# Group weights of dilated attention formed on eight rows, three z tiles beside memory attention, and fetches awaited by their reader

## The reference

```python
for gi, (window, dil) in enumerate(DIL_GROUPS):        # (128, 1), (512, 4), (2048, 16)
    num, m, den = dilated_window_group(q, k, v_a, window, dil)
ms = jnp.stack(ms)
wts = jnp.exp(ms - jnp.max(ms, axis=0, keepdims=True))
num = sum(wts[g][..., None] * nums[g] for g in range(3))
den = jnp.sum(wts * jnp.stack(dens), axis=0)
out = num / den[..., None]
...
y = jnp.concatenate([a_out, b_out, m_out], axis=-1) * jax.nn.silu(z)
return x + y @ w_out
```

## Time and profile before

| | |
|---|---|
| runs | 3665.96, 3662.26, 3666.74 us; median 3665.96 us |
| the profiled execution | 3660.47 us, span 3658.7 us |
| mean granted clock of TensorE over the span | 0.974 |
| busy: PE, DVE, ACT, POOL | 3404.2, 1763.5, 931.8, 1503.5 us |
| share of PE in the chain that ended last | 70%, and DVE 11%, POOL 4%, ACT 3% |

### The profile page before, as it was taken

How to read it: one execution, slowest core, us unless ns; L and a number is a source line. 1 busy time by engine, 2 the same in 40 slices (tenths; PEclk the granted TensorE clock), 3 DMA queues, 4 the chain that set the end, 5 groups by cost and what they waited for, 6 DMA issues and landing times.

```text
span 3658.7 us, 44381 instructions
## 1 busy us (share of the span) xinstructions
PE 3404.2 (93%) x16512; PEld 2766.0 (76%) x16512; DVE 1763.5 (48%) x2626; ACT 931.8 (25%) x1810; POOL 1503.5 (41%) x1917
## 2 busy tenths in 40 slices
PE   7989899999999999989999899889888999999988
PEld 6778888887786677767778588778766777788767
DVE  4734887744124454533523556675544443413343
ACT  3233322213014432323112322323220222300121
POOL 2452533243452245534554254354324334434423
PEclk9999999999999999999999999999999999999999
DMA  3121211121131021231222211010122101211211
GB/s 118 46 81 30 88 40 48 51 64 40 52 101 38 27 67 35 58 109 35 57 55 88 71 41 35 24 35 24 46 68 71 55 21 49 67 40 39 80 36 70
DMA packets 298890, 201.19 MB, mean 55 GB/s; under 512 B 25510, under 2 KB 277418, under 8 KB 298698
## 3 DMA queue, kind: packets, MB, share of 16 engines
q1 hardware_dynamic: 271241, 132.77, 13.2%
q10 hardware_dynamic: 27456, 65.76, 4.9%
HBM read 170.96 MB, written 27.54 MB: 54 GB/s over the span
## 4 chain that ended last, share of the span: by engine, by line
PE 70%; DVE 11%; PEld 6%; POOL 4%; issue 3%; ACT 3%; DMA 1%; ACTq 1%; PEldq 0%; DVEq 0%; POOLq 0%; SPq 0%
PE ps L347 53%; PE ps L1637 4%; PEld ps L347 4%; POOL w_lo L3098 2%; PE ps L987 2%; POOL w_hi L3092 1%; PEld ps L2577 1%; PE ps L360 1%; PE ps L1000 1%; PE ps L2066 1%; ACT wrk L1015 1%; PE ps L1930 1%; PE ps L746 1%; PE ps L2473 1%; PE ps L739 1%
## 5 line engine op out<-in xcount | busy, mean ns | idle before, releaser
L3092 POOL TENSOR_TENSOR w_hi<-w_raw,pool_one 128x256 fp32r<-128x256 f32 x908 | 612.7, 703 | 1996.2 <-PE ps L347 1974.2
L347 PE MATMUL ps<-h_hi,w_hi 128*128 128x512 f32 x2928 | 1206.6, 412 | 77.1 <-POOL w_lo L3098 19.5
L347 PE MATMUL ps<-h_hi,w_lo 128*128 128x512 f32 x2928 | 1152.3, 394 | 0.0
L347 PE MATMUL ps<-h_lo,w_hi 128*128 128x512 f32 x2928 | 1151.5, 393 | 0.0
L3098 POOL TENSOR_TENSOR w_lo<-w_raw,w_hi 128x256 fp32r<-128x256 f32 x1004 | 891.3, 916 | 129.7 <-ACT w_hi L1370 108.4
L347 PEld LDWEIGHTS ps<-h_hi,w_hi 128*128 128x128 f32 x2928 | 557.0, 190 | 250.2 <-issue 92.0
L347 PEld LDWEIGHTS ps<-h_hi,w_lo 128*128 128x128 f32 x2928 | 555.4, 190 | 121.4
L347 PEld LDWEIGHTS ps<-h_lo,w_hi 128*128 128x128 f32 x2928 | 557.9, 191 | 107.0 <-issue 6.0
L347 PE MATMUL ps<-y_hi,w_hi 128*128 128x512 f32 x704 | 289.4, 411 | 33.0 <-DVEq L2644 15.9
L347 PE MATMUL ps<-y_hi,w_lo 128*128 128x512 f32 x704 | 277.9, 395 | 0.0
L347 PE MATMUL ps<-y_lo,w_hi 128*128 128x512 f32 x704 | 277.8, 395 | 0.0
(11 more groups left out here) (400 smaller groups left out, 3961.0 us busy)
## 6 DMA issues: line engine op xcount, KB each, us to landing
w_raw<-in_w_in SPq DMA_DIRECT2D x87, 512.0 KB
w_raw<-in_even_w_in SPq DMA_DIRECT2D x48, 512.0 KB
away<-wrk ACTq DMA_DIRECT2D x72, 256.0 KB, 2.0
w_raw<-in_odd_w_in SPq DMA_DIRECT2D x32, 512.0 KB
wrk<-away ACTq DMA_DIRECT2D x24, 512.0 KB
wrk<-in_x ACTq DMA_DIRECT2D x16, 512.0 KB, 8.7
w_raw<-in_w_br SPq DMA_DIRECT2D x32, 256.0 KB
w_raw<-in_even_w_out SPq DMA_DIRECT2D x24, 256.0 KB
```

Of the source, the lines that this page charges most:

```text
L347: mm = nc.tensor.matmul(ps[:, b, 0:n], w[:, slot, k, :], rhs(part, k, b), start=(k == 0 and q == 0), stop=(k == nk - 1 and q == 2))
L3092: ins = nc.gpsimd.tensor_tensor(hi, raw, one[:, 0:2], ALU.mult)
```

## The change

It has four parts. **One:** in dilated attention the six numbers per token stay on 8 partitions. DVE writes them, multiplied with masks (the new constants low4, high4, low16, high16), into tiles of 128x384; four matmuls bring the maxima and four the sums of all three groups onto 8 rows by 384 columns in token order; maximum, difference, exponential, weighted sum and reciprocal are taken there, and 24 matmuls with the identity's columns as weights spread the finished weights to 128 partitions, where DVE multiplies the three outputs from PSUM. All this stands inside the attention's stage, at planned times behind the last slot; the five stages go, and the join keeps two sums, silu of z and the split. SLOT_TIME goes from 2.7 to 4.2. **Two:** in both layers three of the four z tiles stand beside the memory attention, in `first_gates`: ACT copies the halves out and then applies Silu to three whole tiles, and `gates_beside` has DVE's part. The fourth tile is `last_gate`. **Three:** a fetch is only issued by ACT, and a stage "... there" on the reading engine (PE, for "D x" DVE) waits. **Four:** the mix load moves into the start of the gating's ACT function (`g_act`), and some semaphores are shared.

```diff
-SLOT_TIME = 2.7
+SLOT_TIME = 4.2
...
+    c["low4"] = (i % 32) == np.arange(32)[None, :]
+    c["high4"] = np.concatenate([n8 == 4 * n + i // 32 for n in range(2)], axis=1)
+    c["low16"] = np.stack([((i % 8) == n8) & ((i // 64) == n) for n in range(2)], axis=2).reshape(P, 16)
+    c["high16"] = n8 == (i % 64) // 8
...
+    fetched = sig.sem("fetched")
+
+    def bring(act, dst, src):
+        act.dma_start(dst, src).then_inc(fetched, 16)
+
+    def fetch(name, pairs, us=10.0, before=None, reader="pe"):
 
         def f_act(act):
             for b in range(2):
...
             if before:
                 before(act)
             for tile, place in pairs:
-                load(act, wt(tile), away[place])
-            yield 0.95
-            loads_done(act)
+                bring(act, wt(tile), away[place])
+
+        brought(name, len(pairs), reader)
+
+    awaited = [0]
+
+    def brought(name, n, reader="pe"):
+        awaited[0] += 16 * n
+        count = awaited[0]
+
+        def there(eng):
+            eng.wait_ge(fetched, count)
+        stage(name + " there", 0.1, **{reader: there})
...
+    def first_gates(name, w, first, tiles, free):
+
+        silued = sig.take("z_silued", 3)
+        rs = [run(1, *both(w, first)), run_one(tiles_of(w, first + 2 * P))]
+        where = [(rs[0], 0), (rs[0], 1), (rs[1], 0)]
+
+        def f_pe(pe):
+            for n, r in enumerate(rs):
+                for part in dense_run(pe, r, rhs_h, rhs_h):
+                    yield (2 * n + part * r.n) / 3
+
+        def f_act(act):
+            act.wait_ge(*free)
+            for j, (r, t) in enumerate(where):
+                for b in range(2):
+                    yield (j + (b + 1) / 2) / 3
+                    out_ready(act, r.t0 + t, b)
+                    nc.scalar.activation(wt(tiles[j], b), ps[:, b, :], ACT.Copy).then_inc(dense_free[b], 1)
+            for j, (r, t) in enumerate(where):
+                for b in range(2):
+                    out_taken(act, r.t0 + t, b)
+                nc.scalar.activation(wt(tiles[j]), wt(tiles[j]), ACT.Silu).then_inc(silued.sem, 1)
+        stage(name, 31.2, ("pe",), pe=f_pe, act=f_act)
+        return silued
...
+    def gates_beside(name, o, tiles, silued, taken, us=12.0):
+
+        done = sig.take("y_done", 6)
+
+        def f_dve(dve):
+            ch = chains["dve"]
+            for j in range(3):
+                dve.wait_ge(silued.sem, silued.nth(j))
+                for b in range(2):
+                    yield (2 * j + b) / 6
+                    dve.wait_ge(taken.sem, taken.nth(2 * j + b))
+                    hi = y_hi[:, j, b * HALF:(b + 1) * HALF]
+                    ch.link(nc.vector.tensor_tensor(o(j, b), o(j, b), wt(tiles[j], b), ALU.mult))
+                    ch.link(nc.vector.tensor_copy(hi, o(j, b)))
+                    nc.vector.tensor_tensor(y_lo[:, j, b * HALF:(b + 1) * HALF], o(j, b), hi.bitcast(F32),
+                                            ALU.subtract).then_inc(done.sem, 1)
+        stage(name, us, dve=f_dve)
+        return done
...
+        length = len(slots) + 5.2
...
+            def rows(q):
+                pe.wait_ge(stats_on_dve.sem, (maxima_masked, sums_masked)[q])
+                at = lambda g: ps[0:8, 2 + q, g * P:(g + 1) * P]
+                nc.tensor.matmul(at(0), stats[q][:, 0, :], ident, start=True, stop=True)
+                for n in range(2):
+                    nc.tensor.matmul(at(1), C("high4")[:, 8 * n:8 * n + 8], masked[q][:, n * P:(n + 1) * P],
+                                     start=(n == 0), stop=(n == 1))
+                nc.tensor.matmul(at(2), C("high16"), masked[q][:, 256:384], start=True,
+                                 stop=True).then_inc(stats_on_pe.sem, 1)
+
+            def spread_weights(g):
+                if g == 0:
+                    pe.wait_ge(stats_on_dve.sem, weighed)
+                if g == 2:
+                    pe.wait_ge(taken.sem, taken.nth(11))
+                for u in range(8):
+                    mm = nc.tensor.matmul(ps[:, 2 + 2 * g + u // 4, (u % 4) * P:(u % 4 + 1) * P],
+                                          ident[0:8, u:u + 1].to_broadcast([8, P]), wgt[:, g * P:(g + 1) * P],
+                                          start=True, stop=True)
+                mm.then_inc(stats_on_pe.sem, 1)
...
+            events.append((last + 1.2, last, lambda: rows(0)))
+            events.append((last + 2.2, last, lambda: rows(1)))
+            for g in range(3):
+                events.append((last + 4.0 + 0.3 * g, last, lambda g=g: spread_weights(g)))
...
-            if h == 3:
-                pe.drain().then_inc(last_mixed.sem, 1)
...
+            def maxima_exps():
+                act.wait_ge(stats_on_dve.sem, maxima_less)
+                nc.scalar.activation(wgt, wgt, ACT.Exp).then_inc(maxima_exp.sem, 1)
+            events.append((last + 2.5, last, maxima_exps))
...
+            def mask(q):
+                if q == 1:
+                    dve.wait_ge(expd.sem, expd.nth(11))
+                st = stats[q]
+                nc.vector.tensor_tensor(
+                    masked[q][:, 0:256].rearrange("p (n i r) -> p n i r", n=2, r=4),
+                    st[:, 1, :].rearrange("p (r n) -> p n r", n=2).unsqueeze(2).to_broadcast([P, 2, 32, 4]),
+                    C("low4").unsqueeze(1).unsqueeze(3).to_broadcast([P, 2, 32, 4]), ALU.mult)
+                nc.vector.tensor_tensor(
+                    masked[q][:, 256:384].rearrange("p (i u c) -> p i u c", i=8, c=2),
+                    st[:, 2, :].unsqueeze(1).unsqueeze(3).to_broadcast([P, 8, 8, 2]),
+                    C("low16").rearrange("p (i c) -> p i c", c=2).unsqueeze(2).to_broadcast([P, 8, 8, 2]),
+                    ALU.mult).then_inc(stats_on_dve.sem, 1)
+
+            def less():
+                dve.wait_ge(stats_on_pe.sem, maxima_rows)
+                rows = ps[0:8, 2, 0:384]
+                ch.link(nc.vector.tensor_reduce(joint[:, 0:P], rows.rearrange("p (g t) -> p t g", g=3), AX, ALU.max))
+                nc.vector.tensor_tensor(wgt.rearrange("p (g t) -> p g t", g=3), rows.rearrange("p (g t) -> p g t", g=3),
+                                        joint[:, 0:P].unsqueeze(1).to_broadcast([8, 3, P]),
+                                        ALU.subtract).then_inc(stats_on_dve.sem, 1)
+
+            def weigh():
+                dve.wait_ge(maxima_exp.sem, maxima_exp.nth(0))
+                dve.wait_ge(stats_on_pe.sem, sums_rows)
+                total = joint[:, P:2 * P]
+                ch.link(nc.vector.tensor_tensor(scaled_d, ps[0:8, 3, 0:384], wgt, ALU.mult))
+                ch.link(nc.vector.tensor_reduce(total, scaled_d.rearrange("p (g t) -> p t g", g=3), AX, ALU.add))
+                ch.link(nc.vector.reciprocal(total, total))
+                w3d = wgt.rearrange("p (g t) -> p g t", g=3)
+                nc.vector.tensor_tensor(w3d, w3d, total.unsqueeze(1).to_broadcast([8, 3, P]),
+                                        ALU.mult).then_inc(stats_on_dve.sem, 1)
...
+            events.append((last + 0.7, last, lambda: mask(0)))
+            events.append((last + 1.5, last, lambda: less()))
+            events.append((last + 1.9, last, lambda: mask(1)))
+            events.append((last + 3.0, last, weigh))
+            for g in range(3):
+                events.append((last + 4.4 + 0.3 * g, last, lambda g=g: scale(g)))
...
         def o_dve(dve):
             ch = chains["dve"]
-            for b in range(2):
-                yield b * 0.2
-                ch.link(nc.vector.reciprocal(tmp[:, b * HALF:(b + 1) * HALF], tmp[:, b * HALF:(b + 1) * HALF]))
-            yield 0.4
-            silu_z = y_spare[:, h, :]
+            ch.link(nc.vector.tensor_tensor(out_t[0], out_t[0], out_t[1], ALU.add))
+            ch.link(nc.vector.tensor_tensor(out_t[0], out_t[0], out_t[2], ALU.add))
+            yield 0.35
             for b in range(2):
                 out_taken(dve, r_z.t0, b)
-            for g in range(3):
-                ins = nc.vector.tensor_tensor(out_t[g], out_t[g], wgt[g], ALU.mult)
-            ch.link(ins)
-            ch.link(nc.vector.tensor_tensor(tmp, tmp, silu_z, ALU.mult))
-            yield 0.65
-            ch.link(nc.vector.tensor_tensor(out_t[0], out_t[0], out_t[1], ALU.add))
-            ch.link(nc.vector.tensor_tensor(out_t[0], out_t[0], out_t[2], ALU.add))
-            ch.link(nc.vector.tensor_tensor(out_t[0], out_t[0], tmp, ALU.mult))
-            yield 0.8
+            ch.link(nc.vector.tensor_tensor(out_t[0], out_t[0], y_spare[:, h, :], ALU.mult))
+            yield 0.6
             ch.link(nc.vector.tensor_copy(y_hi[:, h, :], out_t[0]))
-            nc.vector.tensor_tensor(y_lo[:, h, :], out_t[0], y_hi[:, h, :].bitcast(F32), ALU.subtract)
-            dve.drain().then_inc(join_done.sem, 1)
-        stage("maxima spread", 8.0, pe=lambda pe: spread(pe, st_m))
-        stage("maxima copied", 6.0, act=m_act)
-        stage("joint maximum", 9.0, dve=m_dve)
```

(59 more changed lines are left out.)

106 lines of the change are left out of this document (40 added, 66 removed).

## The result

The changed kernel takes 3606.73 us (median of 4 runs, 3601.17 to 3607.47), the kernel before 3664.32 us beside it (4 runs, 3662.26 to 3666.74). The ratio is 0.9839 with a 95% interval of 0.9822 to 0.9856, so 59 us or 1.6% faster. Forecast were 3602 us. The profiled execution of the changed kernel took 3607.19 us, its span is 3605.3 us.

What follows compares the result with a forecast made beforehand. PE was taken as the bound, busy 504.7 of 565 us over the heads. Terms -14 - 45 - 10 + 7 - 2 = -64 us from 3660.5 gave 3596.5, plus 5.5 for the median: 3602 us, range 3570 to 3640.

Steps and rivals of the forecast that it cites:

- the signs named ahead: Out A wait under 2 us, slot waits under 6, no lasting half clock 2200-2700 us, some 10 us wait ending memory attentions.
- PE's own work: Attention heads: 16 fewer small matmuls per head, 64 in all at 0.22 us each, 14 us less.
- Idle time: Attention heads: PE's waits for last join, head changes, silu of z and slots shrink to 7 us, 45 us less.
- The clock: Heads and last join: half clock after four long waits goes with them, 10 us less, bounds 6 and 18.
- The rival with 18 us more for the clock: Clock penalty counted as half the throttled time, idle included: 28 us less instead of 10, total 3584 us; chance 0.08.
- The memory attentions: Both memory attentions: Silu, table loads and gates ahead of the last step make PE wait, 7 us more in both.
- Parts three and four: Fetches worth 0; without the mix load's stage PE's 3.6 us wait for ACT mostly goes, 2 us less.

## Why the prediction was right

The forecast was 64 us against the profiled execution, 3602 us; measured were 53 us from trace to trace and 3606.73 us. Of the signs named ahead all came but one: at the spreads of all four heads the clock was low for 5 to 20 us, where none was to be. By its own terms:

- **PE's own work, -14.** Its busy time in the stretch fell by 7.8 us, and the clock added 9.2 (21.7 against 12.5), so without the clock the work fell by 17. The 0.22 us for a matmul with 8 rows was right at full clock: 270 ns a record against 275. It was the wrong price at half clock.
- **Idle time, -45.** It fell by 50.7. The last wait went from 15.9 to 0.3 where 1 was left, the waits for the join, for silu of z and at the slots went to nothing where 6 were left. What does remain are three waits of 0.7 us at the first spread of a head and small gaps. The chain of small operations just meets its time, as laid out; that it rests on SLOT_TIME, the run at 2.7 shows.
- **The clock, -10.** This step failed, with its sign. It took the low clock to come from long waits alone. Those dips did go; the spreads with 8 rows brought others, and the sum is +9. The prediction had looked at the shape only for the length of the instruction. The rival with 18 us more for the clock failed for the same reason. The price was sound: the run with 128 rows loses nothing over the heads in place of 12.5 us.
- **Out A, 0.** The text had no term for it, and it cost 6.1 us. The prediction said what waits for join_done, but not what had been transferred while the join ran. The transfer of x, moved up, gives 4.6 us of them back by the trace, and the pool weights' load behind it 6.9 more.
- **The memory attentions, +7.** The mechanism was right in its details: a wait of 9.7 us for the last turn (10.4 forecast, though its own times, 12.1 less 1.9, make 10.2), then 1.1. ACT and DVE run as worked out, from the copy of the last half at 2913.56 on:

```profile
2913.56 0.60 ACT L2112 ACTIVATE wrk<-ps 128x512 f32<-128x512 f32 x1 [1.71 <-PE ps L352]
2914.17 1.28 ACT L2116 ACT_TABLE_LOAD   x1
2915.47 2.95 ACT L2116 ACTIVATE wrk<-wrk 128x1024 f32<-128x1024 f32 x3
2918.51 1.28 ACT L1020 ACT_TABLE_LOAD   x1
2919.97 0.47 ACT L1020 ACTIVATE wrk<-ps,small 128x256 f32<-128x256 f32 x1 [0.18 <-DVE small L1056]
...
2916.72 0.69 DVE L2132 TENSOR_TENSOR acc<-acc,wrk 128x512 f32<-128x512 f32 x1 [12.46 <-ACT wrk L2116]
...
2918.52 1.22 DVE L1050 TENSOR_REDUCE small<-ps 128x4 f32<-128x1024 f32 x1
...
2924.23 1.14 DVE L1070 TENSOR_SCALAR wrk<-wrk,small 128x256 f32<-128x256 f32 x4
```

  The sum was too large, since the small waits before the last step are 1.2 us and not 2 to 3 in the even attention: +3.3 and +0.9 by stretches, and within the noise in time. The low clock cost 2.8 us (2.7 forecast), but on the turn and the product behind the wait: the fourth z tile, where it was laid, had 1.00 from 2932.5 us on.
- **Parts three and four, -2.** The wait of 3.6 us went, as forecast, and with it low clock behind it, for which the text had no term: -3.2, and -2.9 us in the next stretch, where the clock cost 3.6 us before and nothing now. PE's wait ahead of L2050 in the first block's memory attention stayed, 2.7 us where it was 2.6.

So two misses of 19 and 6 us were partly made up by 6 us of idle time, 3 each of PE's work and the memory attentions and 4 at the moved load. That these errors had opposite signs is luck. So is a part of the nearness in time: the forecast laid the median 5.5 us above the profiled execution, and beside the changed kernel, whose own lies 0.5 us above its median, that gap was 3.9 us. Between traces the forecast missed by 11 us, between medians by 5.

The Trainium skill, "ScalarE: Activation LUTs", Table sets: the hidden batching unit, says to group activations by table set. The Trainium skill prices each switch there, under What ACT_TABLE_LOAD costs, at 2.66 us with a drain. The trace shows the load, 1.28 us each time, and no drain behind it: the next activation began after 0.02 us. The advice holds all the same: with the Silu tiles behind the last exponentials two loads fewer are made in each attention, where one was expected, and the wait falls from 9.7 to 2.0 us.

## What to carry to other kernels

When a long wait goes, list the transfers that were issued before it ended and the loads queued behind it: they were hidden by it, and may stand in a row. Judge the removal of one in its own stretch of the trace as well as by the time: here moving one gave 4.6 us in out A, and the medians of four runs showed 1; the heads ahead of it took 3 us more in that execution, as much as executions of the same heads differ among themselves. Price a small matmul by what it does to the clock of the dense ones around it, and not by its own length. In an engine with a fixed order, work that is put beside a chain must stand behind the chain's last links; 10 us of PE hung on three activations that nobody yet needed.

## What was not expected of the hardware

With matmuls of 128 columns that contract over 8 rows, an otherwise busy TensorE went from a granted clock of 2.4 GHz to 1.2 GHz: 0.54 and 0.57 in windows of 15 and 20 us in which PE was busy for 14.6 and 19.9 us. With 32 rows the dips stay at three heads of four (0.55 over 15 us); with 128 rows, of which 120 hold zeros, they do not come. So in these runs it went by the rows that the instruction spans, and not by how many of them hold values. Padding with zeros costs a memset for each head and gives 21 us of the heads' stretch, 15 to 18 us of the time.
